# Recurrent layer's inverse: four of its five doubling levels as 32x32 block products instead of 64x64 ones

## The chip, the core and the metric

The kernel runs on one core of a Trainium2 chip. The metric is the device time in microseconds (us) of one execution. A core has TensorE (PE, with its weight loads shown apart as PEld), VectorE (DVE), ScalarE (ACT), GpSimd (POOL) and the queues that start transfers (SP above all). Matrix products read SBUF, write PSUM banks, and are copied back by DVE or ACT. TensorE reads its instructions from memory like any engine: those reads are transfers too, and the trace lists them as a DMA queue of their own ("q8 instruction").

## What is computed

Two transformer blocks over 256 positions of width 2048, all in fp32. The last quarter of the second block is a recurrent layer (`odd_layer` of the reference, RWKV-like): 32 heads of 64 features whose state is updated position by position. It begins

```
def second_block(x, ...):
    for layer in range(DEPTH_2):
        j = layer // 2
        if layer % 2 == 0:
            y = even_layer(x, ev_w_in[j], ev_w_pool[j], ev_pool_scale[j], ev_w_out[j])
        else:
            y = odd_layer(x, od_mu[j], od_w_r[j], od_w_k[j], od_w_v[j], od_w_g[j],
                          od_w0[j], od_w1[j], od_w2[j], od_a0[j], od_a1[j], od_a2[j],
                          od_k_k[j], od_k_a[j], od_r_k[j], od_gn_w[j], od_gn_b[j], od_w_o[j])
        x = layer_norm(DEEPNORM_ALPHA * x + y, ln_g[layer], ln_b[layer])
```

The kernel does not walk 256 positions. It takes the sequence as four chunks of 64, and inside a chunk the updates become one triangular system per head: the inverse of a 64x64 unit triangular matrix is needed, and after that everything is a matrix product. The change is in how that inverse is made.

## The kernel before

One program, unrolled in the part that matters here, with an instruction list for each engine written by hand and tied by semaphores (`await_step` waits for a named step of a named section). Four segments A to D; D is the recurrent layer: first the four projections r, k, v, g, then `pipeline` (L2629), then the output projection.

**The pipeline** goes through `GROUPS` = 8 groups n of four heads (256 features). Each group has ten halves: levels k = 1 to 5, each with a half "Y" and a half "T". All five engines run the same loop `pipeline` with their own functions, so the order of work on each engine is that of the loop: the level's step first, then what `STATE_AT`, `POST_AT`, `SCORE_AT` and the `AHEAD`/`BEHIND` tables (L2621 to L2627) place in that half: the state update of group n-1, the preparation of group n+1 and the normalisation of group n-1.

**The inverse by doubling.** A level k turns an inverse that is right within blocks of 2^k rows into one that is right within blocks of twice that. In `level_pe` (L2389) half Y multiplies the matrix `MB` by the inverse so far `XI` (tile `d_inverse`); `level_vec` (L2420) copies the lower block of each pair, by a mask, into `YI` (tile `d_steps`, prefilled by ACT with identities, L2956); half T multiplies that by the transposed inverse `XT` (tile `d_inverse_turned`, at level 1 `d_first`), `level_act` (L2414) copies the product to SBUF as the new `XT`, and DVE transposes it in 32x32 squares into the new `XI` (L2433). For 64x64 operands a group's 256 positions give two tiles t, and each tile holds two chunks b, one above the other in the partitions, times four heads h. So a half is 16 products of 64x64 by 64x64, on the two diagonal 64x64 tiles of the array (`s` is both the row range and the column range). A product in fp32 appears as two MATMULs and two LDWEIGHTS in the trace. After level 5, `state_pe` (L2470) reads `XT`.

**On TensorE** the halves follow each other as 1Y; 1T, w and xq (L2481); 2Y, sums (L2223, L2226), s (L2508); 2T, p1 (L2536); 3Y, p2, o0 (L2545, L2551); 3T, ru (L2564), turns (L2239); 4Y, turns; 4T, scores (L2359); 5Y, scores, r0; 5T, lora (L2217). In the first group `FIRST_FILL` (L2386) puts products that nobody reads between the halves (L2384).

**SP** loads, for each group, rows and kept projections (`group_rows`, L2142, `group_gate`, L2180), all waiting for `post_pool` "out" of an earlier group, so that thirteen transfers are issued one behind the other.

Of the kernel before, what the change touches and what calls it, by code (L numbers as in the profile page):

```python
# [63 lines left out]
def constant_tables():  # L64
# [20 lines left out]
    for k in range(6):  # L85
        a, b = q >> k, m >> k
        lower = (a == b + 1) & (b % 2 == 0)
        t[f"level{k}"] = (lower if k else (b == a + 1) & (a % 2 == 0)).astype(np.float32)
# [46 lines left out]
def build(nc, a, segments="ABCD"):  # L135
# [4 lines left out]
    PH = 87  # L140
# [1911 lines left out]
    STEPS_I = at("d_steps", [128, 10, 4, 64], F32, PH + 96)  # L2052
    YI = [[STEPS_I[:, 2 * k + t, :, :] for t in range(2)] for k in range(5)]
# [12 lines left out]
    D_TABLES = 9 * 64 + 128 + 6  # L2066
    d_tables = at("d_tables", [128, D_TABLES], F32, PH + 74)
    lev = d_tables[:, 0:6 * 64].rearrange("p (k s) -> p k s", k=6).bitcast(mybir.dt.int32)
    ident_b = d_tables[:, 6 * 64:7 * 64]
    both = d_tables[:, 7 * 64:9 * 64]  # L2070
    centred = d_tables[:, 9 * 64:9 * 64 + 128]
    spans = d_tables[:, 9 * 64 + 128:D_TABLES]
# [15 lines left out]
    if "D" in segments:  # L2088
        for n, (name, w) in enumerate((("r", "od_w_r_2"), ("k", "od_w_k_2"), ("v", "od_w_v_2"), ("g", "od_w_g_2"))):
# [23 lines left out]
            x for k in range(1, 6) for x in (f"{k}Y0", f"{k}Y1", *((f"{k}X0", f"{k}X1") if k < 5 else ()))],  # L2113
# [262 lines left out]

    def level_bank(t):
        return PS[t][:, 0:256].rearrange("p (h s) -> p h s", h=4)

# [9 lines left out]
    def level_pe(pe, n, k, stage):  # L2389
# [6 lines left out]
        for t in range(2):  # L2396
            x = T0[t] if k == 1 else XT[n % 2][t]
# [6 lines left out]
            for h in range(4):  # L2404
                for b in range(2):
                    s = slice(64 * b, 64 * b + 64)
                    if stage == "Y":
                        left, right = MB[n % 2][t][s, h, 0:64], XI[n % 2][t][s, h, :]
                    else:
                        left, right = YI[k - 1][t][s, h, :], x[s, h, :]  # L2410
                    op = pe.matmul(PS[t][s, 64 * h:64 * h + 64], left, right, start=True, stop=True)  # L2411
            op.then_inc(sem("level_pe"), 1)

    def level_act(act, n, k, stage):  # L2414
        if stage == "T":
            for t in range(2):
                await_step(act, "level_pe", f"{k}T{t}", n)
                act.activation(XT[n % 2][t][:, :, :], level_bank(t), ACT.Copy).then_inc(sem("level_act"), 1)

    def level_vec(vec, n, k, stage):  # L2420
        inc = lambda op: op.then_inc(sem("level_vec"), 1)
        flat = lambda x: x[:, :, :].rearrange("p h s -> p (h s)")
        for t in range(2):
            if k == 0:
                continue
            if stage == "Y":
                await_step(vec, "level_pe", f"{k}Y{t}", n)
                if n == 0 and t == 0 and k <= 4:
                    vec.wait_ge(sem("steps_filled"), k)
# [781 lines left out]
```

## Time and profile before

| | us |
|---|---|
| median of 3 runs | 2534.69 |
| lowest, highest | 2532.08, 2538.26 |
| the profiled execution's own time | 2533.41 |
| its span, first to last instruction | 2531.6 |
| the pipeline of eight groups, in that span | about 2180 to 2416 |

The page of the profile gives busy times over the whole span, in which the four large projections and the feed-forward layers dominate: TensorE is busy for 97%. The pipeline is a stage of its own with other limits; what the change is worth has to be read there, from the groups' lengths, the chain of work and the transfers between 2180 and 2416 us.

### The profile page before, as it was taken

Reading aid. Unit: us, or ns where it says so; the run is one execution under the profiler, and the core shown is the slowest. Engines: PE = TensorE matmul, PEld = TensorE weight load, DVE = VectorE, ACT = ScalarE, POOL = GpSimd, SP = SyncE. Lnnn points to the kernel's source line nnn. Section 1 sums busy time; section 2 is a strip of 40 time slices with the busy share of each in tenths; the row PEclk is TensorE's granted clock in tenths of the full one; section 3 lists DMA queues with packets and bytes.
Section 4 is the critical chain, followed back from the end, with each engine's and each line's share of the span. In section 5 each row is a group of like instructions: output and inputs, shape, how many; then the busy total and the mean of one; then the engine's idle time right before and its main releaser. Section 6 shows DMA issues by size and latency. Waiting matters only on the chain.

```text
span 2531.6 us, 39190 instructions
## 1 busy us (share of the span) xinstructions
PE 2464.4 (97%) x16044; PEld 2053.1 (81%) x16044; DVE 1499.4 (59%) x1985; ACT 1251.9 (49%) x1663; POOL 186.5 (7%) x218
## 2 busy tenths in 40 slices
PE   8999999999999999999999999999999999998898
PEld 7886888888888888887888888878788888887786
DVE  5457554584656666666444545445767555687766
ACT  5446444474555555555444444544545445565442
POOL 2002000000000000000000100000000001143330
PEclk9999999999999999999999999999999999999999
DMA  8756666655655555556555655545466677322352
GB/s 264 244 167 134 210 203 203 198 188 188 211 170 196 195 183 179 172 198 233 197 187 197 198 194 183 163 137 173 167 232 218 215 232 251 104 66 62 109 183 101
DMA packets 238570, 462.43 MB, mean 183 GB/s; under 512 B 10064, under 2 KB 32281, under 8 KB 236768
## 3 DMA queue, kind: packets, MB, share of 16 engines
q1 hardware_dynamic: 219280, 421.62, 50.5%
q0 software_dynamic: 18576, 38.28, 5.4%
q8 instruction: 105, 1.72, 0.3%
q10 hardware_dynamic: 576, 0.53, 0.1%
q14 instruction: 33, 0.27, 0.0%
HBM read 445.66 MB, written 14.74 MB: 182 GB/s over the span
## 4 chain that ended last, share of the span: by engine, by line
PE 47%; DVE 4%; ACT 2%; issue 1%; DVEq 0%; ACTq 0%
PE bank L418 12%; PE bank L420 12%; PE bank L419 12%; PE bank L2411 2%; PE bank L2481 1%; DVE d_products L2368 1%; PE bank L2823 1%; PE bank L2508 1%; PE bank L463 0%; PE bank L465 0%; PE bank L464 0%; ACT w_high L268 0%; PE bank L2239 0%; DVE d_steps L2430 0%; PE bank L2545 0%
## 5 line engine op out<-in xcount | busy, mean ns | idle before, releaser
L274 DVE TENSOR_TENSOR w_low<-raw,w_high 128x1024 fp32r<-128x1024 f32 x768 | 929.2, 1222 | 783.8 <-ACT w_high L268 783.0
L268 ACT ACTIVATE w_high<-raw 128x1024 fp32r<-128x1024 f32 x768 | 804.6, 1057 | 911.1 <-PE bank L420 888.1
L418 PE MATMUL bank<-w_high,b_h_high 128*128 128x512 f32 x696 | 272.9, 392 | 0.0
L420 PE MATMUL bank<-w_high,b_h_low 128*128 128x512 f32 x696 | 271.1, 390 | 0.0
L419 PE MATMUL bank<-w_low,b_h_high 128*128 128x512 f32 x696 | 270.8, 389 | 0.0
L418 PE MATMUL bank<-w_high,a_h_high 128*128 128x512 f32 (+1 forms) x632 | 243.8, 386 | 0.0
L420 PE MATMUL bank<-w_high,a_h_low 128*128 128x512 f32 (+1 forms) x632 | 242.8, 384 | 0.0
L419 PE MATMUL bank<-w_low,a_h_high 128*128 128x512 f32 (+1 forms) x632 | 242.7, 384 | 0.0
L418 PE MATMUL bank<-w_high,c_x_high 128*128 128x512 f32 x496 | 195.3, 394 | 0.0
L420 PE MATMUL bank<-w_high,c_x_low 128*128 128x512 f32 x496 | 193.2, 390 | 0.0
L419 PE MATMUL bank<-w_low,c_x_high 128*128 128x512 f32 x496 | 193.0, 389 | 0.0
L418 PE MATMUL bank<-w_high,d_high 128*128 128x512 f32 x448 | 175.4, 392 | 0.0
L419 PE MATMUL bank<-w_low,d_high 128*128 128x512 f32 x448 | 174.4, 389 | 0.0
L420 PE MATMUL bank<-w_high,d_low 128*128 128x512 f32 x448 | 174.3, 389 | 0.0
L420 PEld LDWEIGHTS bank<-w_high,b_h_low 128*128 128x128 f32 x696 | 130.6, 188 | 27.4
L419 PEld LDWEIGHTS bank<-w_low,b_h_high 128*128 128x128 f32 x696 | 130.8, 188 | 26.4
L418 PEld LDWEIGHTS bank<-w_high,b_h_high 128*128 128x128 f32 x696 | 130.7, 188 | 26.4
L420 PEld LDWEIGHTS bank<-w_high,a_h_low 128*128 128x128 f32 x632 | 118.9, 188 | 23.6
L418 PEld LDWEIGHTS bank<-w_high,a_h_high 128*128 128x128 f32 x632 | 119.0, 188 | 23.4 <-issue 0.3
L419 PEld LDWEIGHTS bank<-w_low,a_h_high 128*128 128x128 f32 x632 | 119.0, 188 | 23.3
L418 PE MATMUL bank<-w_high,b_ff_high 128*128 128x512 f32 x344 | 134.3, 390 | 0.9 <-DVE w_low L274 0.8
L420 PE MATMUL bank<-w_high,b_ff_low 128*128 128x512 f32 x344 | 133.9, 389 | 0.0
(463 smaller groups left out, 3782.8 us busy)
## 6 DMA issues: line engine op xcount, KB each, us to landing
raw<-in_w_up SPq DMA_DIRECT2D x88, 1024.0 KB, 5.1
raw<-in_w_in SPq DMA_DIRECT2D x75, 1024.0 KB, 5.2
raw<-in_ev_w_in SPq DMA_DIRECT2D x48, 1024.0 KB, 5.1
raw<-in_w_down SPq DMA_DIRECT2D x44, 1024.0 KB, 5.0
raw<-in_w_out SPq DMA_DIRECT2D x16, 1024.0 KB, 5.0
raw<-in_ev_w_out SPq DMA_DIRECT2D x16, 1024.0 KB, 5.0
raw<-in_od_w_r SPq DMA_DIRECT2D x16, 1024.0 KB, 5.6
raw<-in_od_w_k SPq DMA_DIRECT2D x16, 1024.0 KB, 5.0
```

Of the source, the lines that this page charges most:

```text
L268: act.activation(wh[n % 4][:, :, 0:width], raw_half, ACT.Copy).then_inc(sem("w_high_made"), 1)
L274: vec.tensor_tensor(wl[n % 4][:, :, 0:width], raw_half, wh[n % 4][:, :, 0:width].bitcast(F32), ALU.subtract).then_inc(sem("w_low_made"), 1)
L418: pe.matmul(b, xh, wh[n][:, k % 2, 0:width], start=(c == 0 and k == 0), stop=False)
L419: pe.matmul(b, xh, wl[n][:, k % 2, 0:width], start=False, stop=False)
L420: mm = pe.matmul(b, xl, wh[n][:, k % 2, 0:width], start=False, stop=(c == j.chunks - 1 and k == 3))
L2368: vec.tensor_tensor(MBK[n % 2][:, :, part, h:4:2, :], PS[6 - 2 * part + h][:, :].rearrange("x (p k m) -> x k p m", p=2, k=2), both[:, :].u ...
L2411: op = pe.matmul(PS[t][s, 64 * h:64 * h + 64], left, right, start=True, stop=True)
L2481: op = pe.matmul(PS[bank][s, head(t, h)], left(t, s, h), right(t, s, h), start=(t == 0 and h == 0), stop=True, skip_group_check=True)
L2508: op = pe.matmul(PS[4 + b][half_of(q), col + 64 * p:col + 64 * p + 64], left, right, start=(b, q) not in begun, stop=True, skip_group_chec ...
L2823: mm = pe.matmul(PS[4 + i][0:LORA, 0:S], LW[i][:, k, :], m[:, k, :], start=(k == 0), stop=(k == KT - 1))
```

## The change

Levels 1 to 4 only need products within blocks of 32 rows: the inverse is block diagonal with blocks of at most 32 until level 5 joins the two halves of a chunk.

- `block_products` takes over both halves of levels 1 to 4. Four row ranges of 32 partitions, four heads, two tiles t: 32 products of 32x32 by 32x32 in a half instead of 16 of 64x64, on the four diagonal 32x32 tiles of the array. Results lie in 32 columns per head (`block_bank`).
- The operands of these levels (`YI`, and the new `XI_BLOCKS` and `T_BLOCKS`, tile `d_turned_blocks`) keep 32 columns per head, so DVE's masked copies and transposes and ACT's copies of levels 1 to 4 handle 128x128 instead of 128x256.
- Level 5: half Y multiplies only the off-diagonal 32x32 block (16 products of 32x32, from the upper to the lower partitions of a chunk), half T stays 16 products of 64x64. Its operands are the wide ones again: DVE spreads `T_BLOCKS` into `WIDE` (tile `d_turned_wide`) by two masked copies of 128x256 a group, queued in `level_vec` ahead of the copies of 5Y, and copies 5Y's result into `LAST_I`.
- ACT fills the new constant tiles at the start; the tables of masks have another layout.

Core of the diff:

```diff
@@ -2394,43 +2411,71 @@
         for t in range(2):
-            x = T0[t] if k == 1 else XT[n % 2][t]
...
-            for h in range(4):
-                for b in range(2):
-                    s = slice(64 * b, 64 * b + 64)
-                    if stage == "Y":
-                        left, right = MB[n % 2][t][s, h, 0:64], XI[n % 2][t][s, h, :]
-                    else:
-                        left, right = YI[k - 1][t][s, h, :], x[s, h, :]
-                    op = pe.matmul(PS[t][s, 64 * h:64 * h + 64], left, right, start=True, stop=True)
+            if k < 5:
+                op = block_products(pe, n, k, stage, t)
+            else:
+                for h in range(4):
+                    for b in range(2):
+                        if stage == "Y":
+                            upper, lower = slice(64 * b, 64 * b + 32), slice(64 * b + 32, 64 * b + 64)
+                            op = pe.matmul(PS[t][lower, 32 * h:32 * h + 32], MB[n % 2][t][upper, h, 32:64],
+                                           XI_BLOCKS[n % 2][t][upper, h, :], start=True, stop=True)
+                        else:
+                            s = slice(64 * b, 64 * b + 64)
+                            op = pe.matmul(PS[t][s, 64 * h:64 * h + 64], LAST_I[s, t, h, :], WIDE[s, t, h, :],
+                                           start=True, stop=True)
             op.then_inc(sem("level_pe"), 1)
+
+    def block_products(pe, n, k, stage, t):
+
+        for h in range(4):
+            for i in range(4):
+                s, own = slice(32 * i, 32 * i + 32), slice(32 * (i % 2), 32 * (i % 2) + 32)
+                if stage == "Y":
+                    left = MB[n % 2][t][s, h, own]
+                    right = XI[n % 2][t][s, h, own] if k == 1 else XI_BLOCKS[n % 2][t][s, h, :]
+                else:
+                    left = YI[k - 1][t][s, h, :]
+                    right = T0[t][s, h, own] if k == 1 else T_BLOCKS[0][t][s, h, :]
+                op = pe.matmul(PS[t][s, 32 * h:32 * h + 32], left, right, start=True, stop=True)
+        return op
...
     def level_vec(vec, n, k, stage):
...
+        if k == 5 and stage == "Y":
+            if n == 0:
+                vec.wait_ge(sem("steps_filled"), 5)
+            for t in range(2):
+                inc(vec.copy_predicated(WIDE[:, t, :, :].rearrange("p h (c s) -> p h c s", c=2),
+                                        own_blocks.rearrange("p (c s) -> p c s", c=2).unsqueeze(1)
+                                        .to_broadcast([128, 4, 2, 32]),
+                                        T_BLOCKS[0][t].unsqueeze(2).to_broadcast([128, 4, 2, 32])))
...
-                inc(vec.copy_predicated(YI[k - 1][t], bcast4(lev[:, k, :]), level_bank(t)))
+                inc(vec.copy_predicated(YI[k - 1][t] if k < 5 else LAST_I[:, t, :, 0:32], blocks4(lev[k - 1]),
+                                        block_bank(t)))
...
-                inc(vec.transpose(flat(XI[n % 2][t]), flat(XT[n % 2][t])))
+                inc(vec.transpose(flat(XI_BLOCKS[n % 2][t]), flat(T_BLOCKS[0][t])))
```

TensorE, in the middle of a group, from the end of the state product s over 2T, p1, 3Y, p2 and o0 to 3T. Before (the numbers behind the names are buffers):

```order
L2508 MATMUL bank<-d_products_182,d_solved 64x64 x5
L2411 MATMUL bank<-d_inverse_turned_206,d_steps 64x64 x8
L2411 MATMUL bank<-d_inverse_turned_207,d_steps 64x64 x8
L2536 MATMUL bank<-d_state,d_passed 64x64 x4
L2411 MATMUL bank<-d_inverse_202,d_products_183 64x64 x8
L2411 MATMUL bank<-d_inverse_203,d_products_183 64x64 x8
L2536 MATMUL bank<-d_state,d_passed 64x64 x4
L2545 MATMUL bank<-d_rkvg_166,d_products_182 64x64 x8
L2551 MATMUL bank<-d_removed,d_products_182 64x64 x8
```

And in the changed kernel:

```order
L2553 MATMUL bank<-d_products_182,d_solved 64x64 x5
L2446 MATMUL bank<-d_turned_blocks_208,d_steps 32x32 x16
L2446 MATMUL bank<-d_turned_blocks_209,d_steps 32x32 x16
L2581 MATMUL bank<-d_state,d_passed 64x64 x4
L2446 MATMUL bank<-d_inverse_202,d_products_183 32x32 x16
L2446 MATMUL bank<-d_inverse_203,d_products_183 32x32 x16
L2581 MATMUL bank<-d_state,d_passed 64x64 x4
L2590 MATMUL bank<-d_rkvg_166,d_products_182 64x64 x8
L2596 MATMUL bank<-d_removed,d_products_182 64x64 x8
```

Nothing changes places. Each row of the levels holds twice as many products of a quarter of the work, and 32x32 rows now stand between 64x64 ones. An x8 of this list is sixteen MATMULs and sixteen LDWEIGHTS in the trace.

DVE, from the normalisation of a group to the first scores of the next. Before:

```order
L2433 STREAM_TRANSPOSE d_inverse_202<-d_inverse_turned_206 128x256
L2433 STREAM_TRANSPOSE d_inverse_203<-d_inverse_turned_207 128x256
L2717 RECIPROCAL d_small<-d_small 128x8
L2719 TENSOR_TENSOR d_o<-d_o,d_small 128x512
L2430 COPY_PREDICATED d_steps<-d_tables,bank 128x256 x2
L2368 TENSOR_TENSOR d_products_182<-bank,d_tables 128x2x2x128 x2
```

And in the changed kernel:

```order
L2478 STREAM_TRANSPOSE d_inverse_202<-d_turned_blocks_208 128x128
L2478 STREAM_TRANSPOSE d_inverse_203<-d_turned_blocks_209 128x128
L2762 RECIPROCAL d_small<-d_small 128x8
L2764 TENSOR_TENSOR d_o<-d_o,d_small 128x512
L2463 COPY_PREDICATED d_turned_wide<-d_tables,d_turned_blocks_208 128x256
L2463 COPY_PREDICATED d_turned_wide<-d_tables,d_turned_blocks_209 128x256
L2474 COPY_PREDICATED d_last_steps<-d_tables,bank 128x4x32 x2
L2379 TENSOR_TENSOR d_products_182<-bank,d_tables 128x2x2x128 x2
```

The two spreading copies stand behind the normalisation and ahead of 5Y's copies and of the scores of the next group.

## Rows read from the trace of the kernel before

**Rows 1.** The page's first part: busy time, share, instructions

```profile
PE 2464.4 (97%) x16044; PEld 2053.1 (81%) x16044; DVE 1499.4 (59%) x1985; ACT 1251.9 (49%) x1663; POOL 186.5 (7%) x218
```

**Rows 2.** Stretches: length, busy us (instructions) by engine, granted clock, DMA; seven groups

```profile
core 0: us, PE busy (x) PEld busy (x) DVE busy (x) ACT busy (x) POOL busy (x), PEclk, DMA share, GB/s
2210.58:2239.85 29.27, 26.93 (x750) 24.92 (x749) 25.96 (x59) 17.81 (x33) 8.57 (x7) 1.00 0.22 43
2239.85:2268.08 28.23, 26.01 (x717) 24.02 (x717) 24.28 (x56) 17.55 (x32) 12.94 (x11) 1.00 0.33 80
2268.08:2302.34 34.26, 27.93 (x716) 25.44 (x716) 23.87 (x56) 17.32 (x32) 12.40 (x11) 0.95 0.24 66
2302.34:2331.79 29.45, 26.23 (x716) 24.07 (x716) 23.84 (x56) 17.33 (x32) 12.36 (x11) 1.00 0.27 77
2331.79:2360.66 28.87, 26.28 (x716) 24.07 (x717) 23.52 (x56) 17.22 (x32) 12.87 (x11) 1.00 0.29 78
...
2389.61:2416.36 26.75, 21.91 (x589) 21.18 (x590) 12.51 (x33) 6.74 (x17) 8.51 (x8) 0.81 0.46 160
```

**Rows 3.** The chain that ended last: start, us, what; group 2331.79 to 2360.66

```profile
2331.79 1.15 PE bank L2411 x32
2332.94 1.87 PE bank L2481 x64
2334.81 0.93 PE bank L2411 x32
...
2340.77 0.36 DVE d_inverse L2433
...
2344.43 0.93 PE bank L2411 x30
2345.35 1.23 issue
...
2354.65 0.77 DVE d_steps L2430 x2
```

**Rows 4.** Groups of instructions by shape, 2180 to 2420: count, busy us, mean ns; DVE

```profile
L2430 DVE COPY_PREDICATED d_steps<-d_tables,bank 128x256 f32<-128x256 int32 x80 | 32.5, 438 | 17.2 <-PE bank L2411 15.6 <-ACT d_steps L2956 1.3
...
L2584 DVE TENSOR_TENSOR d_passed<-bank,d_tables 128x128 f32<-128x128 f32 x14 | 3.9, 281 | 0.0
```

**Rows 5.** TensorE in order of time: start, us, what; ru and turns

```profile
2317.68 0.68 PE L2564 MATMUL bank<-d_state,d_read 64*64 64x64 f32 x28
2318.29 0.33 PE L2239 MATMUL bank<-ident,d_query 128*128 128x128 f32 x1
2318.45 0.27 PE L2239 MATMUL bank<-ident,d_t 128*128 128x128 f32 x1
2318.56 0.27 PE L2239 MATMUL bank<-ident,d_minus_b 128*128 128x128 f32 x1
```

**Rows 6.** Stretches as in rows 2: 2210 to 2390, and three inside it

```profile
2210.00:2390.00 180.00, 158.73 (x4335) 145.75 (x4335) 145.85 (x335) 103.23 (x191) 70.66 (x56) 0.99 0.24 62
...
2259.92:2263.40 3.48, 3.48 (x130) 3.48 (x124) 2.39 (x7) 1.76 (x4) 0.00 (x0) 1.00 0.00 0
...
2305.45:2313.55 8.10, 7.78 (x232) 7.31 (x229) 6.70 (x17) 5.25 (x10) 3.81 (x4) 1.00 0.56 147
...
2288.20:2291.50 3.30, 3.30 (x40) 2.85 (x39) 2.54 (x6) 1.19 (x2) 0.00 (x0) 0.50 0.02 5
```

**Rows 7.** Transfers' queue q8: 2210:2390; then 0.1 us from 2284.9, 2288.3, 2305.4, 2313.5

```profile
q8 instruction: 34, 0.56, 1.2%
...
q8 instruction: 1, 0.02, 59.2%
...
q8 instruction: 1, 0.02, 54.8%
...
q8 instruction: 1, 0.02, 62.6%
...
q8 instruction: 1, 0.02, 79.3%
```

**Rows 8.** The chain as in rows 3: TensorE without a releaser, in three groups

```profile
2278.78 1.13 issue
...
2283.44 3.77 issue
...
2314.45 1.72 issue
```

**Rows 9.** SP in order of time: the first and the last of thirteen issues

```profile
2306.86 0.33 SPq L2148 DMA_DIRECT2D d_rkvg<-rkvg  x1
...
2312.80 0.44 SPq L2148 DMA_DIRECT2D d_rows<-in_od_r_k  x1
```

More of the change, by code:

```diff
@@ L84, in constant_tables @@
     q, m = r[:, None] % 64, r[None, :64]
[L85 to L88, printed above, removed]
+    t["level0"] = ((m == q + 1) & (q % 2 == 0)).astype(np.float32)
+    for k in range(1, 5):
+        a, b = (r[:, None] % 32) >> k, r[None, :32] >> k
+        t[f"level{k}"] = ((a == b + 1) & (b % 2 == 0)).astype(np.float32)
+    t["level5"] = np.tile((q >= 32).astype(np.float32), (1, 32))
+    t["ident_rows"] = (r[:, None] % 32 == r[None, :32]).astype(np.float32)
+    t["own_blocks"] = (q // 32 == m // 32).astype(np.float32)
     t["ident_blocks"] = (q == m).astype(np.float32)
@@ L2065, in build @@
     P2 = at("d_p2", [128, 2, GW], F32, PH + 116)
-    D_TABLES = 9 * 64 + 128 + 6
+    D_TABLES = 10 * 64 + 6
     d_tables = at("d_tables", [128, D_TABLES], F32, PH + 74)
[L2068 to L2072, printed above, removed]
+    first_lev = d_tables[:, 0:64].bitcast(mybir.dt.int32)
+    lev = [d_tables[:, 64 + 32 * k:96 + 32 * k].bitcast(mybir.dt.int32) for k in range(5)]
+    ident_rows = d_tables[:, 224:256]
+    own_blocks = d_tables[:, 256:320].bitcast(mybir.dt.int32)
+    ident_b = d_tables[:, 320:384]
+    both = d_tables[:, 384:512]
+    centred = d_tables[:, 512:640]
+    spans = d_tables[:, 640:D_TABLES]
     DSM = at("d_small", [128, 3, 64], F32, PH + 76.78125)
@@ L2112, in build @@
         "level_vec": [
-            x for k in range(1, 6) for x in (f"{k}Y0", f"{k}Y1", *((f"{k}X0", f"{k}X1") if k < 5 else ()))],
+            *(f"{k}{x}" for k in range(1, 5) for x in ("Y0", "Y1", "X0", "X1")), "4W0", "4W1", "5Y0", "5Y1"],
         "state_pe": ["r0", "w", "xq", "s", "p1", "p2", "o0", "ru"],
@@ L2953, in d_act, with fill_steps, fill_last @@
         act.wait_ge(sem("w_used"), 2 * plan["odd_out"].g0)
-        def fill_steps(k, stop):
-            act.activation(STEPS_I[:, 2 * k - 2:2 * stop, :, :].rearrange("p a h s -> p (a h) s"),
-                           ident_b.unsqueeze(1).to_broadcast([128, 8 * (stop - k + 1), 64]), ACT.Copy
+        def fill_steps(k):
+            act.activation(STEPS_I[:, 2 * k - 2:2 * k, :, :].rearrange("p a h s -> p (a h) s"),
+                           ident_rows.unsqueeze(1).to_broadcast([128, 8, 32]), ACT.Copy
                            ).then_inc(sem("steps_filled"), 1)
+        def fill_last():
+            for tile, scale in ((WIDE, 0.0), (LAST_I, 1.0)):
+                act.activation(tile[:, :, :, :].rearrange("p t h s -> p (t h) s"),
+                               ident_b.unsqueeze(1).to_broadcast([128, 8, 64]), ACT.Copy, scale=scale
+                               ).then_inc(sem("steps_filled"), 1)
         def begin(act, half):
             if half == 3:
-                fill_steps(2, 2)
+                fill_steps(2)
                 split_early(act, True)
             if half == 5:
-                fill_steps(3, 3)
-                fill_steps(4, 5)
-        fill_steps(1, 1)
+                fill_steps(3)
+                fill_steps(4)
+                fill_last()
+        fill_steps(1)
         jo = plan["odd_out"]
```

24 lines of the change are left out of this document (17 added, 7 removed).

## The prediction

> **What bounds the kernel now.** Over the whole span TensorE is 97% busy [rows 1], but that is the projections' doing; the change touches only the eight groups of the recurrent pipeline, so I read the stretches of single groups first. A group, counted from one 1T to the next, takes 28.2 to 29.5 us, with one of 34.3 [rows 2]. In it no engine is full: DVE is busy for 24 us, TensorE by its modelled ends for 26. So a group is a chain across engines, and the chain's view comes second [rows 3]: it runs on TensorE without a break through 1T, w, xq, 2Y, sums and s, crosses to DVE, comes back for 3Y, o0 and 3T, and ends on DVE through normalisation, 5Y's copies and the next group's scores. It also holds a piece of 1.23 us that nothing releases ("issue"), in the middle of 3T. That piece is the third thing to look at, because it recurs: 1.13, 3.77 and 1.72 us in two other groups [rows 8].
>
> What ends such a piece? The trace has a queue of instruction transfers. From 2210 to 2390 us it has 34 packets [rows 7], while TensorE executes 4335 MATMULs and 4335 LDWEIGHTS [rows 6]: 8670 / 34 = 255 instructions a packet. (0.56 MB / 34 is 16 KB, 64 bytes an instruction.) TensorE's own program is what this queue carries. Now the times. The packet that starts at 2284.9 fills 59.2% of 16 engines x 0.1 us [rows 7], so it takes 0.95 us and ends at about 2285.9; the idle of 3.77 us that began at 2283.44 ends at 2287.21 [rows 8], 1.3 us later. The packet at 2313.5 takes 1.27 us and ends at 2314.85; the idle of 1.72 us ends at 2316.17 [rows 8], again 1.3 us later. TensorE stood still because its next instructions had not arrived. After it resumed at 2287.21 the next packet started at 2288.35 [rows 7]: 1.15 us to ask, 0.95 to move, 1.3 until it can be executed, **3.4 us a packet** when nothing is in the way; the fastest steady stretch, 254 instructions in 3.48 us [rows 6], fits that. With loads in the way it is longer. SP issues thirteen transfers from 2306.86 to 2313.24 [rows 9], and between the packets of 2305.45 and 2313.55 lie 8.1 us and 461 instructions [rows 6, 7]: asked for after about 255 of them, some 4.5 us in, the packet had to wait about 3.5 us instead of 1.15, and the turnround was about 6. While a packet is asked for only when the one before is entered, TensorE can't execute more than 255 instructions in 3.4 us, or in 6 behind SP's loads.
>
> **The change, part by part.** *The products of levels 1 to 4.* A half now holds 32 MATMULs of 64x64, 0.93 us where TensorE isn't waiting [rows 3], or 29 ns each on two tiles at once, 58 ns a tile. Afterwards 64 MATMULs share four tiles. If half the columns take half the time, that is 64 / 4 x 29 = 0.46 us; if not at all, 0.93. That four tiles do run side by side is in the rows: ru uses the four 64x64 tiles and its 28 MATMULs span 0.68 us, less the last one's 0.22 about 17 ns each [rows 5], below the 29 of two tiles. I take 0.50, a gain of 0.43 (0 to 0.47) a half. On the chain lie 1T, 2Y, 3Y, 3T and 4Y: **-2.15 us a group**. 5Y (as short as the others now), 2T, 4T and 1Y lie beside DVE's work.
>
> *DVE and ACT.* 128x256 takes 438 ns and 128x128 281 [rows 4]: 0.15 less each. On the chain, one transpose (2X), 5Y's two copies, 1Y's first and ACT's copies at 4T: -0.65. The spreading copies are 128x256, 2 x 0.44 = +0.88, and they stand behind the normalisation where DVE is the chain [rows 3]; nothing covers them, since 5Y's result is there by then. **+0.2 us** (-0.2 to +0.4).
>
> *Changing the tile size.* From the 64x64 products of ru to the 128x128 turns the first start comes 0.61 us behind the start of the row, when the last ru has just ended, and the second 0.16 us behind the first, where later ones take 0.11 [rows 5]: about 0.15 us for the change. Before, 1T, w, xq and 2Y were all of one size. New on the chain are 1T to w, xq to 2Y, 3Y to p2, o0 to 3T and 3T to ru: 5 x 0.15, **+0.7 us** (0 to 0.9; the one row I have says that each costs, so I take all five). The Trainium skill ("TensorEngine Tiling (Array Packing)", Key Properties) says that changing the tiling mode, not just the tile, drains TensorE; the rows agree for 64 to 128, none has a 32.
>
> So the engines' own work makes a group 1.25 us shorter (2.2 to 0): about 27.0 where it was 28.2. The first group, with its fills, gains about as much. If that were all: 8 x 1.25 = 10 us off, 2523.
>
> *The instructions.* A group has 716 MATMULs [rows 2], 1432 instructions with the weight loads, 5.6 packets. Each half of levels 1 to 4 adds 32 MATMULs, level 5 none in sum: + 8 x 32 = 256, so 972 MATMULs, 1944 instructions, **7.6 packets** a group, 16 more over the eight. At 3.4 us each they need 25.9 us of a group that should take 27. SP's loads lengthen one or two of them by about 3 us (issue of 6.4 us, landing later, against the same TensorE work as now): +4.5 us, 30.4. And the packets can't be spread evenly: from 4T to 1Y DVE sets the pace for about 9.5 us, in which TensorE has only 592 instructions, 2.3 packets or 7.9 us; 1.6 us of the queue's time is lost there. **32 us a group** where loads are in the way. Before, the same sum was 5.6 x 3.4 + 3 = 22 us of 29: only the local pieces of 1.1 to 1.7 us showed.
>
> Group by group against [rows 2]: 28.2 to 32 (+3.8); the one of 34.3, which already stood still twice and ran at half clock, stays (0; up to +3); 29.45 and 28.87 to 32 (+2.5, +3.1); the next like it, which is the stretch left out there, +3.0; the last, 26.75, has four large weight loads in its way, +3.3. The group from 2210 has only seven small loads: -1. The first has sixteen loads and fills, +1.5. Together +16. Standing still also costs clock: behind the 3.77 us the granted clock was 0.50 [rows 6], the lower level of 1.2 GHz, for 3.3 us in which TensorE ran only 40 MATMULs. Some groups will see that again, though TensorE then waits for instructions anyway: +2. The profiled execution took 2533.4, 1.8 more than its span and 1.3 under the median; 2533.4 + 18 = **2552 us**.
>
> **The rivals.** *The packets stay hidden* (faster, 0.22). The gain of 10 us comes out: 2523. For it: from 2259.92 on TensorE ran 254 instructions in 3.48 us without standing still, and most packets cost nothing visible. It needs either that the next packet is asked for earlier than I read, or that two can be under way. The Trainium skill ("Runtime: NRT & Kernel Launch", Instruction fetch mechanics) describes the 16 KB blocks and calls the fetch hidden, since dispatch is slower than the refill; by that rule this rival wins. The pieces of [rows 8] speak against it for this kernel.
>
> *The stall eats the gain and no more* (same, 0.13). If only the one packet behind SP's loads matters, TensorE gets to it earlier and waits until the same moment, about 13.8 us behind 1T in the group of 2302.34: what 1T, 2Y and 3Y gained is given back, what 4Y and 4T gained is spent on the spreading copies. 2534.
>
> *Two late packets and half clock* (slower, 0.15). 461 instructions lasted 8.1 us under SP's loads; TensorE would now want to execute about 780 in that time. If two packets in a row wait as long, a group takes 34 to 35, and each pause of 4 us brings 3.3 us at 0.50: +6 a group over six groups, 2572.
>
> *The blocks don't do what they are for* (slower, 0.05). If 32 columns take 58 ns a tile as 64 do, the levels gain nothing on TensorE, and with tile changes and spreading copies a group is 0.9 longer even with all packets hidden: 2541; with the packets it is nearly the forecast, because these bind anyway.
>
> **How the numbers follow.** The forecast itself, packets every 3.4 us and one and a half late ones a group, has 0.45: 2552, own range 2541 to 2562. Slower by over 0.2% (5 us, about what a measurement of this kernel tells from none) is 0.45 + 0.15 + 0.05 = 0.65, same 0.13, faster 0.22. The range leaves out the outer half of the first rival and the end of the third: 2521 to 2574.
>
> **What would show it.** Between 2210 and the end of group seven, more packets in the instruction queue, by two a group, still 255 instructions apart. More and longer "issue" pieces in TensorE's chain, each ending 1.3 us behind the end of a packet: 3 to 5 us instead of 1 to 2, and new ones where no loads are. In stretches where TensorE runs on, 32-column halves of 0.5 us. Transposes and copies of levels 1 to 4 at about 0.29 us. DVE less busy, TensorE less busy, groups longer. I am wrong if packets come closer than 3.4 us apart, if groups shorten to 27 us, or if an added packet costs nothing although it comes late.

## The result, and the profile after

The changed kernel takes 2556.35 us (median; 2555.04 to 2556.7), the kernel before beside it 2535.05 (2532.08 to 2538.26): a ratio of 1.0093, 95% interval 1.008 to 1.0106. It is slower by about 21 us. The forecast was 2552, slower.

The page of the changed kernel, busy time by engine and the queue of instruction transfers (packets, MB, share of 16 engines):

```profile
PE 2463.3 (96%) x18092; PEld 2046.6 (80%) x18092; DVE 1484.6 (58%) x2001; ACT 1245.2 (49%) x1665; POOL 185.0 (7%) x218
...
q8 instruction: 121, 1.98, 0.3%
```

The same queue on the page of before:

```profile
q8 instruction: 105, 1.72, 0.3%
```

Against [rows 1], every engine is a little less busy, and the span is 22.8 us longer (2554.4 against 2531.6). TensorE executes 18092 - 16044 = 2048 more MATMULs, eight times 256, and the instruction queue carries 16 packets more. Where is the time? The stretches from one 1T to the next, of the changed kernel (length, busy us and instructions of each engine, granted clock, share of the DMA engines, GB/s):

```profile
2180.17:2212.15 31.98, 25.79 (x749) 23.03 (x748) 17.90 (x42) 16.48 (x33) 6.66 (x7) 0.84 0.50 113
2212.15:2241.73 29.58, 24.57 (x972) 21.70 (x972) 21.87 (x58) 16.41 (x32) 7.94 (x7) 1.00 0.15 40
2241.73:2273.72 31.99, 25.92 (x972) 23.13 (x972) 21.65 (x58) 16.57 (x32) 12.33 (x11) 0.95 0.27 71
2273.72:2307.68 33.96, 26.84 (x973) 24.01 (x973) 21.80 (x58) 16.62 (x32) 12.36 (x11) 0.90 0.29 68
2307.68:2341.79 34.11, 28.33 (x972) 24.99 (x973) 22.29 (x58) 16.68 (x32) 12.38 (x11) 0.85 0.29 67
2341.79:2376.32 34.53, 27.20 (x973) 24.02 (x973) 22.44 (x58) 16.47 (x32) 12.34 (x11) 0.90 0.25 67
2376.32:2409.09 32.77, 24.70 (x965) 22.33 (x965) 22.29 (x58) 14.71 (x30) 11.11 (x10) 0.90 0.11 28
```

Beside [rows 2]: a group has 972 MATMULs, DVE has 2 us less to do (22.3 for 24), and yet the group is longer; the granted clock, 1.00 in most groups before, is 0.84 to 0.95 here in six of the seven stretches. The chain that ended last, in the group from 2307.68 and the next (start, us, what), says where the length is:

```profile
2307.68 0.75 PE bank L2446 x50
2308.43 2.01 PE bank L2526 x64
...
2318.02 0.40 PE bank L2590 x13
2318.42 3.17 issue
2321.59 0.36 PE bank L2590 x2
...
2351.56 0.26 PE bank L2446 x6
2351.82 3.96 issue
2355.78 1.05 PE bank L2446 x58
...
2357.46 0.85 PE bank L2590 x16
```

L2446 is the line of the 32x32 products. A half of levels 1 to 4, 64 MATMULs of this shape, takes 0.75 us where 32 of 64x64 took 1.15 or 0.93 [rows 3] (the chain's view counts some of the 64 elsewhere: x50). But TensorE stands still in the middle of 3Y or of o0 with nothing that releases it, for 3.17 and 3.96 us, where [rows 8] had 1.72 at the most in a group that did not already run long. Behind such a piece the work itself is slow: 16 MATMULs of o0 take 0.85 us at a granted clock of 0.50, and 0.47 at full clock in the kernel before. The piece at 2318.42 can be followed to its cause. SP's issues around it (start, us), the first and the last of thirteen:

```profile
2312.34 0.33 SPq L2159 DMA_DIRECT2D d_rkvg<-rkvg  x1
...
2319.12 1.56 SPq L2159 DMA_DIRECT2D d_rows<-in_od_r_k  x1
```

The instruction queue in the 0.1 us from 2319.1:

```profile
q8 instruction: 1, 0.02, 75.3%
```

A packet starts there; 75.3% of 16 engines x 0.1 us make 1.2 us of transfer. It ends at 2320.3, and TensorE goes on at 2321.59, 1.3 us later, as before. The packet ahead of it began at 2313.0: 6.1 us apart, in the middle of SP's thirteen loads. For the piece of 3.96 us the same times are 2354.25 for the packet's end and 2355.78 for TensorE, 1.5 us later.

### The profile page after: what moved, and what is told of

It reads as the page before. It is cut to its first block, busy times and chain, and to the rows that moved or that the text cites. A ratio compares the mean times of both kernels' runs of the same rounds, so it can differ in the third digit from the quotient of the medians.

```text
span 2554.4 us, 43305 instructions
## 1 busy us (share of the span) xinstructions
PE 2463.3 (96%) x18092; PEld 2046.6 (80%) x18092; DVE 1484.6 (58%) x2001; ACT 1245.2 (49%) x1665; POOL 185.0 (7%) x218
## 4 chain that ended last, share of the span: by engine, by line
PE 47%; DVE 3%; issue 2%; ACT 2%; DVEq 0%; ACTq 0%
PE bank L421 12%; PE bank L423 12%; PE bank L422 12%; PE bank L2446 1%; PE bank L2526 1%; PE bank L2250 1%; PE bank L2553 1%; DVE d_products L2379 1%; PE bank L2868 1%; PE bank L2596 0%; PE bank L2590 0%; PE bank L466 0%; PE bank L468 0%; PE bank L467 0%; ACT w_high L271 0%
## 5 line engine op out<-in xcount | busy, mean ns | idle before, releaser
L423 PEld LDWEIGHTS bank<-w_high,b_h_low 128*128 128x128 f32 x696 | 130.6, 188 | 27.4
L422 PE MATMUL bank<-w_low,b_ff_high 128*128 128x512 f32 x344 | 133.9, 389 | 0.0
```

Source lines behind the costliest of these rows:

```text
L422: pe.matmul(b, xh, wl[n][:, k % 2, 0:width], start=False, stop=False)
L423: mm = pe.matmul(b, xl, wh[n][:, k % 2, 0:width], start=False, stop=(c == j.chunks - 1 and k == 3))
```

## The experiments

Three theories were held against each other. **Packets**: TensorE is held up because 1944 instructions a group need 7.6 packets, each with a turnround of 3.4 us or more. **Clock**: standing still a little lowers the granted clock, and the slow clock is what costs. **Blocks**: 32x32 tiles, mode changes and the spreading copies are slow in themselves. Eleven kernels were run. The kernel before, run again beside each set, moved by 3.3 us between sets (2531.7 to 2535.1), so differences between sets are good to about that.

The last two columns add up each trace between 2170 and 2480 us. "Held up" is the time that late packets take on the chain: pieces of 0.3 us or more that nothing releases and behind which the chain goes on with TensorE. In all thirteen kernels each such piece ends 1.2 to 1.6 us behind the end of a packet. "Half clock" is the time with a granted clock of 0.50, the level of 1.2 GHz.

| kernel | us | MATMULs a group | packets | held up, us | half clock, us |
|---|---|---|---|---|---|
| before (beside the others) | 2531.7 to 2533.7 | 716 | 105 | 11.6 | 17 |
| changed | 2556.4 | 972 | 121 | 31.8 | 61 |
| changed, levels 1 to 4 in one pass | 2521.8 | 716 | 105 | 12.6 | 58 |
| before, levels 1 to 4 in one pass | 2518.0 | 588 | 97 | 2.3 | 44 |
| before, levels 1 to 5 in one pass | 2519.1 | 556 | 95 | 0.7 | 61 |
| changed, small loads | 2537.3 | 972 | 121 | 24.3 | 34 |
| before, small loads | 2520.9 | 716 | 105 | 2.1 | 14 |
| changed, one pass and small loads | 2515.2 | 716 | 105 | 5.0 | 55 |
| changed, loads spread | 2555.7 | 972 | 121 | 27.4 | 51 |
| before, 512 instructions more a group | 2593.6 | 972 | 121 | 15.2 | 48 |
| before, 128 instructions more, as long | 2559.2 | 780 | 109 | 6.8 | 0 |
| changed, long products added | 2581.2 | 988 | 122 | 29.3 | 55 |
| changed in one pass, long products added | 2553.1 | 732 | 106 | 8.6 | 58 |

From before to changed, the time held up grows by 20.2 us, of a span that grows by 22.8. The half clock grows by 44 us, and on the chain TensorE works at it for 53.7 us instead of 16.4; work that took 37.3 us at half clock would take at least half of that at full clock, so this is worth up to 19 us more. By this estimate the engines' own work became 13 to 16 us shorter (the lower end prices the clock as at the end of this section). The two losses go together: between 2240 and 2400 us the clock falls five times, four times in the last 1.1 us of a held-up piece of 3.2 to 4.0 us, once 0.4 us behind one of 2.2.

**Half the instructions at the same place.** Each product of levels 1 to 4 is made of the upper 16 bits of its operands (one pass), and so has one MATMUL and one weight load instead of two of each. In `block_products`:

```diff
+                high = lambda x: x.bitcast(mybir.dt.bfloat16)[:, 1::2]
-                op = pe.matmul(PS[t][s, 32 * h:32 * h + 32], left, right, start=True, stop=True)
+                op = pe.matmul(PS[t][s, 32 * h:32 * h + 32], high(left), high(right), start=True, stop=True)
```

> The changed kernel, with each product of levels 1 to 4 made of the upper 16 bits of its operands, so that it is one pass instead of two: two instructions (weight load and MATMUL) instead of four, at the same place, in the same tile mode, with the same waits. The inverse comes out less precise. A group has 972 - 512 / 2 x 1 = 716 MATMULs again or fewer (512 of its MATMULs become 256), 1432 instructions, 5.6 packets. If packets of instructions are what lengthened the groups, the pieces without a releaser in TensorE's chain shrink to what they were before the change, the packets of the whole kernel return to about 105, the groups take 26 to 28 us, and the kernel about 2515 to 2525: faster than the kernel before by 10 to 20. If the lost clock is the cause (TensorE stands still more, is granted 0.50 more often and then does everything at half speed), this kernel, in which TensorE has still less to do, sees at least as much time at 0.50 and stays above 2540. If 32x32 tiles or the mode changes are slow in themselves, it stays above 2540 too, with few pieces without a releaser.

Measured: 2521.82 us, ratio to before 0.9954 (0.9938 to 0.9971), 105 packets, within the 2515 to 2525 expected if packets are the cause. That is 34.5 us under the changed kernel with the same blocks, mode changes and copies. Its stretches (columns as above), three of them:

```profile
2232.70:2261.72 29.02, 23.86 (x718) 21.16 (x718) 22.93 (x58) 16.28 (x32) 13.28 (x12) 0.88 0.28 78
2261.72:2292.78 31.06, 23.58 (x716) 20.64 (x717) 22.10 (x58) 16.11 (x32) 11.57 (x10) 0.89 0.27 73
2292.78:2321.62 28.84, 24.32 (x716) 21.34 (x717) 23.28 (x58) 16.10 (x32) 12.35 (x11) 0.88 0.32 78
```

The groups are 3 to 5 us shorter than the same ones of the changed kernel, with about the same clock (0.88 to 0.89 against 0.85 to 0.95) and about the same time at half clock (58 against 61 us). So the lost clock is not what makes the changed kernel slow on its own, and neither are the blocks. Of the 34.5 us, 19.2 are late packets (31.8 against 12.6), and at most 5.6 are the clock (42.6 against 53.7 us of TensorE's work on the chain). The other 10 or so are the halves themselves, which one pass shortens too: 3Y from 0.75 to 0.46 us, 3T from 0.68 to 0.30. The chain of this kernel:

```profile
2301.68 0.46 PE bank L2447 x31
...
2306.16 0.30 PE bank L2447 x32
```

**The loads cut, in both kernels.** For groups from the fourth on, 16 of the 128 rows are loaded, in `load` as shown and in `group_gate` in the same way. The other rows keep an older group's data, so these kernels leave out a part of the work and serve as probes only:

```diff
         def load(out, src, what):
+            if n >= 3:
+                out, src = out[0:16], src[0:16]
             sp.dma_start(out, src)
```

> The changed kernel, with the group loads of SP (groups from the fourth on) cut to 16 of their 128 rows; the rest of each tile keeps an older group's data. The number of transfers and their places stay, their bytes shrink to an eighth. If it is the loads in the DMA queues that hold up the packets, their spacing behind SP's thirteen transfers falls from 6 us or more towards 3.4, and a group of 1944 instructions takes 27 to 29 us (7.6 packets x 3.4 = 26): from the fourth group on 5 x 4 = 20 us less, some 2535. If it is not the bytes but SP's issuing of thirteen transfers, or if the instruction packets are not what bounds a group, the groups stay at 32 to 34 us and the kernel at 2550 or more.

> The kernel before, with SP's group loads cut to 16 of 128 rows in the same way. It is the control for the one above: a group of 1432 instructions needs 5.6 x 3.4 = 19 us of 28, so the packets cost little without loads. If loads hurt only through the packets, the group of 34.3 us shrinks to about 28 and the others by 1 us at most: 6 to 10 us less than the kernel before, about 2527. If the loads' bytes also slow something else, such as the waits for the loaded rows, both kernels gain the same 15 to 20 us and their difference stays at 20.

Measured: 2537.32 for the changed kernel (19 us less) and 2520.93 for the one before (about 13 less). Two stretches of the changed kernel with small loads, then two of the kernel before with them:

```profile
2239.66:2269.33 29.67, 24.81 (x973) 21.87 (x973) 22.98 (x58) 16.80 (x32) 12.38 (x11) 1.00 0.06 14
2299.82:2329.21 29.39, 25.11 (x973) 21.75 (x973) 21.77 (x58) 16.48 (x32) 12.36 (x11) 1.00 0.06 14
```

```profile
2237.24:2265.27 28.03, 25.85 (x717) 23.98 (x717) 24.47 (x56) 17.43 (x32) 12.84 (x11) 1.00 0.05 13
2293.30:2321.33 28.03, 25.85 (x717) 23.98 (x717) 24.47 (x56) 17.43 (x32) 12.82 (x11) 1.00 0.05 13
```

This is the cleanest pair of the study: hardly any load traffic, the clock at 1.00 in all four. Before, five stretches in a row take 28.03 us to the hundredth: nothing is late. The changed kernel takes 29.4 to 30.5, so it is 1.4 to 2.5 us longer even with nothing in the packets' way. Its chain in the group from 2299.82:

```profile
2299.82 0.75 PE bank L2449 x50
2300.57 2.01 PE bank L2529 x64
2302.58 0.68 PE bank L2449 x50
...
2310.30 0.40 PE bank L2593 x13
2310.70 1.11 issue
...
2312.14 0.41 PE bank L2599 x14
...
2314.23 0.38 PE bank L2612 x13
2314.61 0.96 issue
2315.56 0.56 PE bank L2612 x19
```

Two pieces without a releaser, 1.11 and 0.96 us, where the kernel before with small loads has none over 0.5 in any of these stretches. Without them (and a piece of 0.34 ahead of the sums) the group would be about 27.0. The loads then add 4 us or so to a group of the changed kernel (29.4 to 30.5 against 34), 0.1 to 1.4 to most groups of before and 6.2 to the one of 34.3, of which the two pieces of 1.13 and 3.77 in [rows 8] are 4.9. What the loads do to a packet can be seen behind a late one. With small loads the next packet begins 1.1 to 1.4 us after TensorE goes on, in 21 of 24 cases. In the changed kernel that is so in 11 of 19; in the others it takes 1.6 to 3.8 us. Both of the expectation's readings are half right: the loads hurt both kernels, and by more where there are more packets; the difference of the two kernels falls from about 21 to 16 us. The kernel before gained more than its forecast (about 2527).

**The loads spread.** SP waits for 2T, 3T, 4Y and 4T of the group two ahead, for example:

```diff
-            await_step(sp, "level_pe", "1T1", n - 2)
+            await_step(sp, "level_pe", "3T1" if n >= 3 else "1T1", n - 2)
```

> The changed kernel, with SP's group loads (groups from the fourth on) spread over the group by three waits on the levels of the group two ahead: the loads that stood in one row of thirteen go out at 2T, 3T, 4Y and 4T. Same bytes, same number. If a packet is late because it queues behind a row of transfers, the two packets of 6 us or more become three or four of 4 to 4.5, and a group shrinks by 1 to 3 us: 2538 to 2550. If only the sum of bytes counts, nothing changes (2556). If the loads come late, the groups get longer by waits on SP's transfers, and the kernel is over 2560.

Measured: 2555.66, ratio to before 1.0092 (1.0075 to 1.0109), as without it. In the trace the thirteen loads go out from 2312.07 to 2328.87 in place of 2312.34 to 2319.12, though eight of them still within 5.7 us. Single groups moved both ways (30.6 to 33.5 us; this trace is of the fastest execution, 2550.97), the median not. The forecast of 2538 to 2550 was wrong: taking the row of loads apart this far does not bring the packets back, and since the first eight still stand together it does not refute that a row of loads delays one. Loads spread evenly weren't tried.

**Instructions added to the kernel before.** Ahead of the products of each stage from 2Y to 5T, for both tiles t. The first has many short products, the second few long ones:

```diff
+            for j in range(8):
+                s = slice(64 * (j % 2), 64 * (j % 2) + 64)
+                pe.matmul(PS[t][s, j:j + 1], ident_b[s, 0:64], ident_b[s, j:j + 1], start=True, stop=True)
```

```diff
+            for b in range(2):
+                s = slice(64 * b, 64 * b + 64)
+                pe.matmul(PS[t][s, 0:256].rearrange("p (c s) -> p c s", c=2), ident_b[s, 0:64],
+                          both[s, 0:128].unsqueeze(1).to_broadcast([64, 2, 128]), start=True, stop=True)
```

In their expectations a half is one tile t (16 MATMULs); the prediction called both together a half.

> The kernel before, with eight extra one-column products of 64x64 tiles ahead of each half of levels 2 to 5, into columns that the half itself overwrites: 16 halves x 8 products x 4 instructions = 512 a group, as many as the change adds, 1944 in all, with no 32x32 tile, no new mode and no spreading copy. TensorE's own work grows by 16 MATMULs a half, 0.25 to 0.45 us where a half is on the chain (five of them: 1.2 to 2.2 us a group, 10 to 18 us in all). If packets bind, the packets of the whole kernel become 121, groups under loads take 32 to 35 us, and the kernel is 25 to 45 us longer: 2560 to 2580. If instructions are free, it is the 10 to 18 us alone, the same as in its companion with long products.

> The companion: the same halves are preceded by two products of 256 columns in place of eight of one column, so TensorE works about as long (4 MATMULs of about 110 ns a tile pair, 0.45 us or so a half) on a quarter of the instructions: 16 x 8 = 128 more a group. If packets bind, this kernel is faster than the one with many short products although its TensorE is at least as busy: 10 to 20 us over the kernel before, with 109 packets. If TensorE's time is what counts, it is as slow as the other or slower.

Measured: 2593.57 (ratio 1.0243, 1.0216 to 1.0269) and 2559.17 (1.0096, 1.0075 to 1.0117). The two are alike in the time they take of TensorE: from the start of the first added MATMUL to the start of the first one behind them are 439 ns with 16 short ones and 434 with 4 long ones (medians of the undisturbed cases). Not quite alike, though: the half's own products then take longer behind the short ones, which makes 0.98 us in all for a tile's added and own products, against 0.95. I had counted five places on the chain; with both tiles there are ten, 4.3 us a group, so both kernels came out longer than expected. What tells is the difference. First the kernel with short products, then the one with long ones:

```profile
2247.78:2285.69 37.91, 34.73 (x972) 33.29 (x972) 24.01 (x56) 17.61 (x32) 12.35 (x11) 0.91 0.23 61
2285.69:2320.57 34.88, 33.20 (x972) 31.49 (x972) 23.93 (x56) 17.61 (x32) 12.34 (x11) 1.00 0.25 66
```

```profile
2248.48:2281.92 33.44, 32.20 (x781) 28.81 (x781) 23.76 (x56) 17.59 (x32) 12.38 (x10) 1.00 0.24 68
2281.92:2314.06 32.14, 32.06 (x781) 28.77 (x781) 24.48 (x56) 17.59 (x32) 12.38 (x10) 1.00 0.25 71
```

And the instruction queues of their pages, in the same order:

```profile
q8 instruction: 121, 1.98, 0.3%
```

```profile
q8 instruction: 109, 1.79, 0.3%
```

384 more instructions a group, for nearly the same time of TensorE, make the kernel 34.4 us longer. Nothing of the change is in these kernels, no 32x32 tile, no mode change, no copy. But 34.4 us is not the price of 12 packets alone. The groups with long products, all at 1.00, take 32.1 to 34.1 us; with short ones the group at 1.00 takes 34.9, those at 0.87 to 0.96 take 37.9 to 40.0. The chains of the two groups at 1.00 that are shown, first with short products, then with long ones, say what the 2.7 us between them are:

```profile
2289.13 0.52 PE bank L2412 x16
...
2299.55 1.12 issue
...
2304.20 0.48 issue
```

```profile
2300.38 0.46 PE bank L2412 x16
```

1.6 us are two late packets, and most of the rest is TensorE's own: 0.52 us for 0.46 behind the short products. Over the whole trace, late packets are 8.4 us more (15.2 against 6.8), TensorE's own work 4 to 9 us more (0.035 us a tile, or the 1.1 us left of this group), and the rest goes with the half clock: 48 us of it, where the kernel with long products has none.

**What the blocks are worth when packets bind less.** The kernel before in one pass (levels 1 to 4, with the same `high`), and the changed kernel in one pass with small loads:

> The kernel before, with the products of levels 1 to 4 in one pass of the upper 16 bits, still 64x64 blocks: 128 MATMULs fewer a group, 588 in all, 1176 instructions, 4.6 packets. It is the partner of the changed kernel in one pass (2521.8): both have packets to spare or nearly so, and what is left between them is the blocks' own effect on the engines (halves half as long on TensorE, transposes and copies 0.15 us shorter, two spreading copies and the mode changes more). By my sum the blocks are worth 1.25 us a group, less about half of the 2.15 us on TensorE since one-pass halves are short anyway: near 0. Then this kernel gives 2510 to 2520 and beats the other, because it has 256 instructions a group less. If the blocks' work on the engines is worth as much as the change's idea says, it is at 2525 or above.

> The changed kernel with both: levels 1 to 4 in one pass of the upper 16 bits, and SP's group loads from the fourth group on cut to 16 of 128 rows. Nothing should be left in the way of instructions; a group is then what the engines need. With loads cut alone the changed kernel's steady group took 29.4 to 30.5 us, the kernel before 28.03. If the packets' turnround of 3.4 us x 7.6 is what held the former, this one takes 25.5 to 27 a group and the kernel about 2508 to 2515. If 29.5 us is the engines' own (mode changes, spreading copies), it takes 28 or more, 2520 and above.

Measured: 2518.01 (ratio 0.9939, 0.9918 to 0.996), as expected, and 2515.23 (0.9921, 0.99 to 0.9942), at the upper end of 2508 to 2515. Two stretches of the first, then three of the second:

```profile
2263.05:2293.03 29.98, 25.32 (x588) 23.32 (x588) 24.88 (x56) 17.39 (x32) 12.35 (x11) 0.83 0.32 75
2293.03:2320.61 27.58, 22.64 (x588) 20.57 (x588) 24.59 (x56) 17.16 (x32) 12.82 (x11) 0.94 0.28 81
```

```profile
2259.58:2288.87 29.29, 25.04 (x716) 22.52 (x717) 23.83 (x58) 16.32 (x32) 13.42 (x12) 0.83 0.05 13
2288.87:2315.82 26.95, 23.00 (x716) 20.03 (x716) 22.72 (x58) 16.43 (x32) 11.78 (x10) 0.94 0.06 15
2315.82:2345.17 29.35, 25.39 (x717) 22.71 (x717) 23.49 (x58) 16.44 (x32) 12.36 (x11) 0.83 0.05 13
```

At the same clock (0.94) a group takes 27.6 us with 64x64 products and 26.9 with blocks, 0.65 less. The two differ in their loads too, which cost a group of the kernel before 0.1 to 0.2 us where nothing was late (28.11 and 28.23 against 28.03), so the change's idea is worth about 0.5 us a group. It is less on the mean: from the second stretch on, six of them average 27.8 with blocks and 28.0 without, because two of the six with blocks are at 0.83 and one of the others. The kernel before with both, one pass and small loads, wasn't run. With the loads as they are it is not had: 2521.8 for the blocks (716 MATMULs), 2518.0 for the old tiles (588). The second of these is the fastest of the kernels that do all their loads; it costs the lower 16 bits of every operand of levels 1 to 4.

**Fewer instructions still.** Level 5 of the kernel before in one pass too:

> The kernel before, with level 5 in one pass too: 556 MATMULs a group, 4.4 packets, 64 instructions fewer than with levels 1 to 4 in one pass (2518.0). Its steady group took 27.6 us there, and its TensorE was not on the chain at 5T. If packets still cost something, 2513 to 2517; if 27.6 us a group is the engines' chain, 2517 to 2519, the same. The inverse is less precise by one more level.

Measured: 2519.14 (ratio 0.9945, 0.9929 to 0.9962), 95 packets, no gain. Five of its groups took 28.3 to 29.8 us at clocks of 0.83 to 0.94, most of its partner's 27.6 at 0.94. Of late packets there were 0.7 us left, where the partner had 2.3, but the half clock grew from 44 to 61 us: less work of TensorE went with a lower clock.

**The clock.** One product of 128x128 and 256 columns was put ahead of each tile's products at 4T, 5Y, 5T and 1Y, to keep TensorE at work:

```diff
+            if (k, stage) in ((4, "T"), (5, "Y"), (5, "T"), (1, "Y")):
+                pe.matmul(PS[t][:, 0:256].rearrange("p (c s) -> p c s", c=2), centred,
+                          centred.unsqueeze(1).to_broadcast([128, 2, 128]), start=True, stop=True)
```

> The changed kernel, with one long product (128x128, 256 columns, 4 instructions) ahead of each half of 4T, 5Y, 5T and 1Y, into columns that the half overwrites or that nobody reads: 8 a group, 32 instructions more, 7.7 packets. They keep TensorE at work where it waits for DVE; what they are for is the granted clock, which was 0.50 for 61 us of the changed kernel's pipeline against 17 of before. Their own cost is 0.9 us a half where it is on the chain (1Y's first at the most, and 4T's), 1 to 2 us a group. If the lost clock is a cause beside the packets, the time at 0.50 falls and the kernel comes down by 5 to 15 us in spite of them: 2540 to 2550. If packets alone are the cause, it does not gain: 2556 to 2570.

> The changed kernel in one pass (2521.8; 58 us at 0.50 in the pipeline), with the same long products. Here packets bind less and 0.50 should cost more of its own, since TensorE's work lies on the chain. If the clock matters, the groups that took 29 to 31 us go to 27 to 28 and the kernel to 2510 to 2518. If not, it is at 2522 to 2532, by the long products' own time.

Measured: 2581.22 (ratio 1.0183, 1.0159 to 1.0206) and 2553.12 (1.0075, 1.0052 to 1.0098), 25 and 31 us more than without, above every figure expected. I had priced the long products wrongly, at 1 to 2 us a group: on the chain they take 36 and 43 us in all. Time at half clock hardly fell, from 61 to 55 us in the first and from 58 to 58 in the second, so these two decide nothing on the clock.

What the clock costs can be read elsewhere, in the one-pass stretches above: a group at 0.83 is 2.4 us longer than one at 0.94. In the three groups at 0.83 no late packet is on the chain, and they were at half clock for 10.2 us in place of 3.4. So 6.8 us more at half clock cost 2.4 us, where DVE and ACT hold much of the chain; where TensorE holds it, 16 MATMULs of o0 took 0.85 us for 0.47. Here the clock falls without a late packet ahead of it. So two of the three theories hold for the changed kernel, late packets first and the clock as a second loss. That its five falls stand at the held-up pieces speaks for the packets as their cause; no run separates the two.

## Why the prediction came out as it did, by its steps

**Sign, cause and number of packets: right.** 7.6 packets a group, sixteen more in all; the pieces without a releaser grew to 3.17 and 3.96 us and ended 1.3 and 1.5 us behind a packet, and the 6 us behind SP's loads are there (2313.0 to 2319.1). The first rival, packets hidden, is refuted by the 31.8 us held up in the changed kernel. By the Trainium skill ("Runtime: NRT & Kernel Launch", Instruction fetch mechanics) the fetch is hidden, since dispatch is slower than the refill. The groups of the kernel before with small loads agree with it, 5.6 packets each and no late one; at 7.6 packets a group, or behind SP's loads, these runs contradict it.

**The size: in part luck.** Of the 18 us forecast, the engines' own work was -10, the packets +26 and the clock +2. The traces give about -13 to -16, +20 and up to +19 (+16 at 2.4 us for 6.8). The packets cost less than forecast and the clock much more, and the two misses cancel. Which of the packets' terms was too high, the 4.5 us for SP's loads or the 1.6 for uneven work, wasn't separated.

**The products of levels 1 to 4: mis-sized.** I took 0.50 us for a half, a gain of 0.43. The chain shows 0.75 and 0.68 where it was 1.15 and 0.93: 0.40 for 1T, 3Y and 4Y (1.08 to 0.68), 0.25 for 2Y and 3T, -1.7 us a group and not -2.15. 64 MATMULs in 0.68 to 0.75 us are 11 to 12 ns each, 43 to 47 a tile, against 58 with 64 columns. Half the columns took three quarters of the time and more, not half. So the fourth rival was partly true.

**DVE and ACT: right.** By shape, between 2180 and 2420 (count, busy us, mean ns), beside [rows 4]:

```profile
L2478 DVE STREAM_TRANSPOSE d_inverse<-d_turned_blocks 128x128 f32<-128x128 f32 x60 | 16.0, 294 | 25.1 <-ACT d_turned_blocks L2454 24.6
L2474 DVE COPY_PREDICATED d_steps<-d_tables,bank 128x128 f32<-128x128 int32 x59 | 16.0, 296 | 27.3 <-PE bank L2446 25.8 <-ACT d_steps L3001 1.1
L2463 DVE COPY_PREDICATED d_turned_wide<-d_tables,d_turned_blocks 128x256 f32<-128x256 int32 x14 | 5.4, 439 | 0.0
```

296 and 439 ns, where 0.29 and 0.44 us had been forecast.

**Changing the tile size: about right, rather more.** w takes 2.01 us where it took 1.87, the sums behind 2Y 1.33 (two pieces, with small loads, and 0.34 between them) where they took 1.06: 0.14 and 0.27. Without its idle pieces the group of the changed kernel with small loads is 27.0, as the prediction's sum of the engines' own work had it; the smaller gain on TensorE must have been made up elsewhere on the chain, which wasn't followed. Over all eight groups the gain was 13 to 16 us by the estimate above, more than the 10 forecast.

**The turnround of a packet: mis-sized.** 3.4 us is near the fastest: the closest packets of each kernel are 3.2 to 3.6 us apart (3.3 in the changed one, so the sign "closer than 3.4" was just seen). But the usual turnround is longer. Behind a late packet, where the next one is asked for at once, the distance to the next is 3.7 us with small loads (median of 21, 3.5 to 4.2) and 3.55 in the changed kernel (median of 11). With small loads the transfer takes 1.2 us and the way to TensorE 1.4 (medians), where I had read 0.95 and 1.3. The same sum with 3.7 gives 7.6 x 3.7 + 1.6 = 29.7 us, and a group with small loads took 29.4 to 30.5. I had 25.9 + 1.6. The median distance of all packets, 3.9 us, says nothing by itself: with 255 instructions in each it only repeats the group's length.

**The clock: mis-sized.** I took +2 us in all, on the ground that TensorE then waits for instructions anyway. It was at half clock for 61 us instead of 17, 54 of them with its own work on the chain, which is worth 16 to 19 us by the estimates above. This is the term of the sum that was furthest off.

**Group by group.** The forecast was 32 us where loads interfere. The group from 2241.73 took 31.99; the one that took 34.26 before took 33.96 (0 forecast); the tail from the last 1T grew by 3.3 (3.3 forecast). The groups from 2307.68 and 2341.79 grew by 4.7 and 5.7 where I had 2.5 and 3.1: they hold pieces of 3 to 4 us and a clock of 0.85 and 0.90, which is the third rival in part. The next one, from 2376.32, grew by 3.8 (3.0 forecast). The group from 2212.15, with few loads, became 1.5 us longer, not 1 shorter: the slower packets alone. The first stretch grew by 2.5 (1.5 forecast). In return the first 1T came 2.1 us earlier, which I had left out. Together 22.8 us of span against 18.

## What to carry to other kernels

Splitting a product into smaller ones that share the array is paid in instructions as well as in time: count them per stretch, and compare with what the instruction queue delivers in that stretch (here 255 in 3.3 us at best, 3.5 to 3.7 as a rule, 6 behind a row of loads). When the count comes near that, a form with fewer instructions (one pass, a wider product) is worth more than one with less work per instruction, and the pieces in TensorE's chain that nothing releases are the place to look. Look at the granted clock behind them too: here it cost nearly as much as the waits themselves.

## What the runs showed of the hardware that I had not expected

- 384 instructions more a group for nearly the same TensorE time (0.98 us a tile with its own products, against 0.95) cost 34.4 us in a kernel of 2.5 ms: 8 us in late packets, 4 to 9 in TensorE's own time, the rest with a half clock that the other kernel never had.
- In the changed kernel the five falls of the clock between 2240 and 2400 us came in the last 1.1 us of a piece of 3.2 to 4.0 us in which TensorE had no instructions, or 0.4 us behind one of 2.2. In the one-pass kernels, where TensorE had less to do, the clock fell without such a piece.
- On four diagonal tiles a 32-column fp32 MATMUL took 43 to 47 ns a tile, a 64-column one on two tiles 58.
- With the loads cut, the kernel before repeated a group five times at 28.03 us; with them, groups took 28.1 to 34.3. 4.9 of the 6.2 us in the longest group are pieces in which TensorE had no instructions.
- The kernel with the fewest instructions (95 packets) was no faster than one with 97, and was at half clock for 61 us between 2170 and 2480, as long as the changed one.
